# Prompt's dilated attention: copies of one unit between the next unit's exponentials, and one copy in four made by VectorE

## What is computed

```python
def dilated_group_prompt(q, k, v, dilation, span, slopes):
    ...
    s = jnp.einsum("znqhe,znkhe->znhqk", qb, kb).astype(jnp.float32) * scale
    s = s - slopes[:, None, None] * (dist * dilation).astype(jnp.float32)
    s = jnp.where(valid[None, :, None], s, NEG_INF)
    m = jnp.max(s, axis=-1)
    e = jnp.exp(s - m[..., None])
    den = jnp.sum(e, axis=-1)
    o = jnp.einsum("znhqk,znkhe->znqhe", e, vb.astype(jnp.float32)).reshape(z, nb * span, H, E)
    ...

def merge_groups(parts):
    M = functools.reduce(jnp.maximum, [m for _, m, _ in parts])
    num = sum(o * jnp.exp(m - M)[..., None] for o, m, _ in parts)
    den = sum(dn * jnp.exp(m - M) for _, m, dn in parts)
    return num / den[..., None]
```

## Time and profile before

| | |
|---|---|
| median of 3 runs | 1567.02 us |
| lowest, highest | 1566.27, 1567.53 us |
| the profiled execution's own time | 1569.71 us |
| its span, first to last instruction | 1567.9 us |
| its mean granted TensorE clock | 0.974 |
| TensorE busy: matmuls, weight loads | 1461.7 us (93%), 1354.0 us (86%) |
| VectorE, ScalarE, GpSimd busy | 673.4 us (43%), 467.1 us (30%), 612.9 us (39%) |
| the stage of the change, from the first scores to the spreading of the shares | 1068.69 to 1145.48 us of the span |

### The profile page before, as it was taken

One profiled execution on the slowest core, in us unless ns is written; L12 is line 12 of the kernel. 1 busy time (PEld: TensorE's weight loads), 2 busy tenths in 40 slices (PEclk: granted clock), 3 DMA queues, 4 the chain that ended last, 5 costly groups with the idle time before them and its releaser, 6 DMA issues.

```text
span 1567.9 us, 28214 instructions
## 1 busy us (share of the span) xinstructions
PE 1461.7 (93%) x12103; PEld 1354.0 (86%) x12103; DVE 673.4 (43%) x984; ACT 467.1 (30%) x866; POOL 612.9 (39%) x276
## 2 busy tenths in 40 slices
PE   6969995888999999999999999998879999999998
PEld 6857763555899999999999999887669999999998
DVE  4668776777254400233113454425665420034212
ACT  4215544343332221122322111114633221122322
POOL 1412213342336644466343443231024654366441
PEclk9979997999999999999999999999989999999999
DMA  4234854675243544454433674558923444544421
GB/s 158 76 101 164 296 172 178 243 280 211 84 162 135 194 155 138 154 190 142 154 141 102 215 250 134 171 187 267 315 90 135 144 151 143 205 134 144 151 81 55
DMA packets 124060, 258.80 MB, mean 165 GB/s; under 512 B 7257, under 2 KB 104681, under 8 KB 117697
## 3 DMA queue, kind: packets, MB, share of 16 engines
q1 hardware_dynamic: 117824, 219.73, 41.1%
q0 software_dynamic: 6144, 37.75, 6.5%
HBM read 249.87 MB, written 95.58 MB: 220 GB/s over the span
## 4 chain that ended last, share of the span: by engine, by line
PE 86%; DVE 8%; issue 2%; ACT 2%; another core or an unknown queue 0%; DMA 0%; SPq 0%; POOL 0%; DVEq 0%; ACTq 0%
PE ps L539 23%; PE ps L543 23%; PE ps L540 22%; PE ps L846 4%; PE ps L748 2%; PE ps L867 1%; ACT sc L2276 1%; DVE KT L1566 1%; PE ps L795 1%; PE ps L1051 1%; PE ps L763 1%; PE ps L1085 1%; PE ps L952 1%; PE ps L887 1%; PE ps L728 1%
## 5 line engine op out<-in xcount | busy, mean ns | idle before, releaser
L2328 POOL TENSOR_TENSOR whl<-wraw,whl 128x2048 fp32r<-128x2048 f32 (+3 forms) x127 | 448.6, 3541 | 539.0 <-ACT whl L1975 539.0
L539 PE MATMUL ps<-hA,whl 128*128 128x260 f32 x1216 | 323.4, 287 | 11.1 <-POOL hA L2328 6.0
L540 PE MATMUL ps<-hA,whl 128*128 128x260 f32 x1216 | 318.6, 283 | 0.0
L1975 ACT ACTIVATE whl<-wraw 128x2048 fp32r<-128x2048 f32 (+3 forms) x127 | 186.1, 1486 | 424.6 <-PE ps L543 397.4
L539 PE MATMUL ps<-uT,whl 128*128 128x260 f32 x1024 | 268.4, 283 | 0.0
L540 PE MATMUL ps<-uT,whl 128*128 128x260 f32 x1024 | 266.3, 281 | 0.0
L543 PE MATMUL ps<-hA,whl 128*128 128x260 f32 x1216 | 247.4, 285 | 0.0
L539 PEld LDWEIGHTS ps<-hA,whl 128*128 128x128 f32 x1216 | 231.5, 190 | 14.5 <-issue 12.8
L540 PEld LDWEIGHTS ps<-hA,whl 128*128 128x128 f32 x1216 | 232.0, 191 | 0.1
L543 PE MATMUL ps<-uT,whl 128*128 128x260 f32 x1024 | 206.7, 283 | 0.0
L540 PEld LDWEIGHTS ps<-uT,whl 128*128 128x128 f32 x1024 | 193.2, 189 | 0.0
(11 more groups left out here) (303 smaller groups left out, 1991.9 us busy)
## 6 DMA issues: line engine op xcount, KB each, us to landing
out_ds<-in_state SPq DMA_DIRECT2D x32, 2047.0 KB, 10.4
wraw<-in_w_up SPq DMA_DIRECT2D x32, 1024.0 KB, 5.6
wraw<-in_w_down SPq DMA_DIRECT2D x32, 1024.0 KB, 5.1
wraw<-in_w_qkv SPq DMA_DIRECT2D x18, 1024.0 KB, 5.2
out_ds<-in_state SPq DMA_DIRECT2D x8, 2044.0 KB, 12.3
dv<-in_state SPq DMA_DIRECT2D x36, 256.0 KB, 5.3
dv<-q_scratch SPq DMA_DIRECT2D x6, 1024.0 KB, 6.2
wraw<-in_w_omla SPq DMA_DIRECT2D x4, 1024.0 KB, 11.2
```

The source lines that it names most:

```text
L539: pe.matmul(ps[:, 2 * u + a, 0:HALF], hi(k), rhs(k, 0)[:, c], start=first, stop=False)
L540: pe.matmul(ps[:, 2 * u + a, 0:HALF], hi(k), rhs(k, 1)[:, c], start=False, stop=False)
L1975: ins = act.activation(dst(0), src, ACT.Copy)
L2328: return pool.tensor_tensor(dst, src, hi.bitcast(F32), ALU.subtract)
```

## The change

- ScalarE's loop runs one step longer. Between the exponentials of unit k it makes the copies of unit k-1: after part 0's exponentials copy 0, after part 1's copy 1, after part 3's copy 3.
- Copy 2 of each unit is made by VectorE (`d_third`), for unit k-2 between the two heads' reductions of unit k's maxima; those of the last two units follow at the end. It has a semaphore of its own, and `wait_taken` lets TensorE's turns and values wait for the right one.
- TensorE issues the scores of three units ahead of the first turn, and those of unit k+3 between values 1 and turn 3 of unit k. The statistics are turned earlier.
- VectorE's outputs (`d_out`) come one unit later, and so does `shares`.

No instruction is added or removed on TensorE; eight copies go from ScalarE to VectorE.

```diff
@@ tensor @@
+            def wait_taken(n):
+
+                k, j = divmod(n, 4)
+                if j == 2:
+                    pe.wait_ge(dil_third_taken, k + 1)
+                else:
+                    pe.wait_ge(dil_turn_taken, 3 * k + min(j, 2) + 1)
...
                 if n >= 2:
-                    pe.wait_ge(dil_turn_taken, n - 1)
+                    wait_taken(n - 2)
...
-                pe.wait_ge(dil_turn_taken, n + 1)
+                wait_taken(n)
...
-            d_scores(0)
+            for k in range(3):
+                d_scores(k)
             for k in range(DU):
-                if k + 1 < DU:
-                    d_scores(k + 1)
                 d_turn(k, 0)
-                if k == DU - 1:
-                    for a in range(2):
-                        pe.wait_ge(dil_biased[a], DU)
-                    turn_stats(0, top)
                 for j in range(4):
                     if j < 3:
                         d_turn(k, j + 1)
-                    if k == DU - 1 and j == 2:
+                    if k == DU - 1 and j == 0:
+                        pe.wait_ge(dil_exp, 8 * DU)
                         turn_stats(1, total)
                     d_values(k, j)
+                    if j == 1 and k + 3 < DU:
+                        d_scores(k + 3)
+                    if j == 1 and k == DU - 2:
+                        pe.wait_ge(dil_max_ready, DU)
+                        turn_stats(0, top)
@@ vector @@
                 for a in range(2):
                     h = 2 * p + a
+                    if a and k >= 2:
+                        d_third(k - 2)
...
+            def d_third(k):
+
+                n = 4 * k + 2
+                dve.wait_ge(dil_turned, n + 1)
+                if n >= 4:
+                    dve.wait_ge(dil_values_used, n - 3)
+                two = lambda x: x.rearrange("p (a c) -> p a c", a=2)
+                dve.tensor_copy(two(scT[:, n % 4, :]), two(ps[:, 4 + n % 2, :])).then_inc(dil_third_taken, 1)
...
-            for k in range(DU + 2):
+            for k in range(DU + 3):
                 if k < DU:
                     d_max(k)
-                if k == DU + 1:
+                if DU <= k < DU + 2:
+                    d_third(k - 2)
+                if k == DU + 2:
                     shares()
-                if k >= 2:
-                    d_out(k - 2)
+                if k >= 3:
+                    d_out(k - 3)
@@ scalar @@
-            for k in range(DU):
+            for k in range(DU + 1):
                 for j in range(4):
-                    d_exp(k, j)
-                for j in range(4):
-                    d_taken(k, j)
-                    if k == DU - 1 and j == 2:
-                        share_exp()
+                    if k < DU:
+                        d_exp(k, j)
+                    if k and j != 2:
+                        d_taken(k - 1, j)
+                if k == DU - 1:
+                    share_exp()
```

More of the change, by code:

```diff
@@ L330, in program @@
         dil_turn_taken = semaphore("dil_turn_taken")
+        dil_third_taken = semaphore("dil_third_taken")
         dil_values_used = semaphore("dil_values_used")
```

## The result

| | before | after |
|---|---|---|
| median of 5 runs each | 1567.35 us (1566.27 to 1569.35) | 1559.20 us (1557.76 to 1560.29) |
| ratio, 95% interval | | 0.9947 (0.9935 to 0.9960) |
| profiled execution: time, span, granted clock | 1569.71, 1567.9 us, 0.974 | 1560.29, 1558.4 us, 0.972 |

The kernel is 8.2 us faster. To a gain above 5.4 us the prediction had given a chance of 0.01.

What follows compares the result with a forecast made beforehand. TensorE was taken to bound the kernel, waiting in turn with ScalarE. In the stage, 4.1 us from waits plus 1.2 from low clock gave 5.4, less 0.7: 1567.02 - 4.7 = 1562.3 us, range 1559.8 to 1565.8 (8 in 10).

Steps and rivals of the forecast that it cites:

- a gain above 5.4 us: Whole kernel: more gained than the upper bound of 5.4 us, the end being shorter; chance 0.01.
- Work and waits of the old stage: First scores to spreading of the shares, 76.79 us: TensorE's work 59.8, waits 15.7, low clock 1.2.
- Waits of the new stage: TensorE in the new order: 6.3 start, 2.2 units 1 to 4, 1.7 units 5 to 7, 1.3 end; 11.5 in all.
- the walk: Following the new order through the stage with durations from the old profile, to find TensorE's waits: 11.5 us, stage 71.3.
- The 4.1 us by waits: Part of the stage's 5.4 us shortening that comes from fewer TensorE waits.
- Low clock at the start: Stage's start: a second wait of 2.5 us may halve TensorE's clock, costing up to 1.2; 0.7 taken off the gain.
- Low clock of before: Old stage, unit 3: values and turns took 3.55 us against 2.34 in unit 5; 1.2 us counted as gained.
- What follows the stage moves with it: Behind the stage: everything starts earlier by the stage's gain, with no gain of its own.
- The third copy: Copy 2 on VectorE: takes 0.68 us, bounds 0.6 to 1.1, covered by TensorE's time per unit.
- The weights: Next weights, a possible stop: land about 1142.6 us, used at 1170.96; 5 us earlier is still late enough.
- S: Rival theory of the experiments: something at the stage's start or ahead of it; the stage began 2.9 us earlier.

Runs made afterwards that it cites:

- the fillers of the start: Changed kernel with 14 small transposes behind each of the first two scores; 1558.72 us, ratio to before 0.9942.
- the filled kernel: Kernel before, its order kept, with small transposes of the identity in all longer waits of the stage; 1560.93 us, ratio 0.9962.
- both fillers: Changed kernel with 14 transposes behind each of the first two scores, 13 ahead of the projection, and shares ahead of unit 6's output; 1558.30 us, 0.9940.
- its variant with the longer copy: Changed kernel with VectorE's copy 2 made four times in a row, slot about 2.8 us instead of 0.6; 1567.30 us, ratio 0.9999.

## Why the prediction was wrong

- **Work and waits of the old stage (59.8 + 15.7): right.** With the longer waits filled and the full clock it took 75.60.
- **Waits of the new stage (11.5, so 71.3): right.** 71.36 without low clock. The waits are where the walk put them: 2.50 before unit 2's scores, 0.25 and 0.21 in the middle (foretold 0.16 and 0.30), 0.40 in unit 5 (0.5), 1.19 at the end (1.3). The 4.1 us by waits stand (15.7 less 11.5 is 4.2; the prediction had 4.1).
- **Low clock at the start (0.7 off): right in kind, short in size.** It is 1.1: 72.48 less 71.36. The Trainium skill (TensorE: Matmul & The Clock Gate, "Why this matters for your kernels") says to leave no long gaps between bursts of matmuls, or the clock falls back; I had weighed it and given it only this term. The stage's start agrees with it (waits of 2.36 and 2.50, then 10 us at 0.50), and the fillers of the start agree too. The prediction told the rule without the word long, and in the middle the trace goes beyond the page: three of the four waits of 1.79 us left open were followed by half clock.
- **Low clock of before (1.2, "from the low clock in unit 3"): the step that failed.** The term was mis-sized: I counted the low stretches that one profiled execution showed inside the stage, and took that as the kernel. The waits of 1.7 to 1.8 us in units 3, 5 and 7 can each be followed by half clock: unit 3 was in both profiles of before, unit 5 in one of the two, unit 7 in neither, but in the one with units 3 and 5 filled. Fillers, with the order left as it was, are worth 6.3 us in the timed runs, for the stage and what follows it. No profile shows all of that at once. An estimate from the profiles: against 75.60, units 3 and 5 cost 2.6 together (78.21) and unit 7 1.8 (77.40), and behind the stage before is 1.5 to 2.3 longer than the filled kernel (next point). If all fell together, that would be 5.9 to 6.7. So my 1.2 stands for up to 4.4 in the stage, and the rest is a term that I had put at nothing.
- **"What follows the stage moves with it": this step failed too.** It was put at nothing and became shorter, in most executions. From the spreading to the end (the span less the spreading's start) it is 422.4 and 421.6 us in the two profiles of before and 421.9 with units 3 and 5 filled; 420.1, 420.1 and 420.3 in the three of the changed kernel; and 420.1 in before with all fillers. The clock goes with it: in the 20 us from the spreading on it was 0.66 in both profiles of before and 0.74 in the first of the changed kernel. But it varies by execution here too: two variants with the new order, the fillers at the start and both fillers, have 421.8 and 421.7, and the one with only ScalarE's order changed has 420.0. The spreading's own matmuls took 3.71 us in the first profile of before, but 2.03 in the second, and take 2.41, so they are no part of the change:

```profile
1146.39 2.03 PE L1125 MATMUL ps<-sq,rope 8*128 8x256 f32 x32 [1.61 <-DVE sq L1905]
```

The 13.72 us behind the spreading's start, in the first profiles of before and after:

```profile
1145.48:1159.20 13.72, 7.94 (x50) 6.94 (x50) 10.44 (x13) 2.55 (x4) 4.98 (x4) 0.51 0.01 2
```

```profile
1138.28:1152.00 13.72, 7.11 (x55) 6.05 (x56) 10.45 (x13) 2.54 (x4) 5.14 (x4) 0.63 0.30 124
```

- **The third copy (0.68, hidden): right, 0.68 to 0.69.** That it gains nothing itself I had not said; the run with all copies on ScalarE showed no gain of it.
- **The weights: right.** They stopped nothing.

The sum as the runs have it, on the third chip: 6.3 from the clock by fillers and 3.3 from the order in the timed runs, where the profiles have 4.1 from waits less 1.1 at the start, 3.0. That is 9.3 to 9.7, and 9.7 was measured. A check by the low-clock time is coarse. On the first chip the median fell from 97.5 to 84.4 us, 13.1 x 0.365 = 4.8, and with 4.1 that is 8.9 of the 10.3 measured; but with the slopes of the other chips the 4.8 would be 3.2 or 4.1, and on the third chip the filled kernel's fall from 90.8 to 65.5 gives 25.3 x 0.314 = 7.9 where 6.3 was measured.

What stays open: which stretches of before were slow in the timed runs was not seen, only their sum. On the first chip the two profiled executions differ by 8.2 us, and the profiles place it: 5.7 in the stage, 1.5 behind it, 0.9 ahead of it. The timed gain is 10.3, larger by 2.1, since the profiled execution of before (1569.86 us) lay 4.0 below its median and that of the changed kernel (1561.66) 1.8 below. Ahead of the stage the program is the same in all kernels, and yet the stage began between 1060.8 and 1069.3 us. Some of that is again the clock: on the third chip the changed kernel began it at 1060.79 with a granted clock of 0.83 between 95 and 112 us, and its variant with the longer copy at 1064.40 with 0.63. The 2.9 us of the first pair of profiles are not explained by this, since there before had 0.82 and after 0.51. A part of S of about 1 us is not excluded.

## What to carry to other kernels

Count the cost of a wait of TensorE twice: its own length, and the stretch at half clock that may follow. Take the second from several executions or from the mean clocks of the timed runs, since one profile shows one execution. To see how much of a gain is clock, fill the waits of the old kernel with matmuls of no use; that separates the two at the cost of one run. In this kernel moving copies between exponentials paid only with the scores moved further ahead (36 us slower without), and moving work to an idle engine brought nothing that could be measured, since order was the limit.

## What the runs showed of the hardware

- The even scores (256 columns) took 1.79 us at full clock and 3.36 at half, but the odd scores (128 columns, strided) took 4.12 and 4.13, also at the start, where the granted clock over them was 0.69 (1069.95 to 1074.08), that is, at half for six tenths of the time: something other than TensorE's clock limits them.
- Filler of 2.6 us ahead of the projection left the clock at half, filler of 4.7 us brought it up; in the waits of the stage, fillers of 0.9 to 1.8 us kept it up.
- In four profiles with the new order, the changed kernel's third among them, TensorE stopped near the stage's end with no releaser, for 0.68, 0.83, 1.50 and 2.83 us; no profile with the old order of TensorE has such a stop. The state copies were running; what the cause is was not tested.
